# Hybrid decoder trunk: every gated mixture turned by VectorE squares and DRAM or made already turned, sparse half of the output projection first

## The reference, cut to what matters

```python
h = rms_norm(x, pre_w)
dq, dk, dv, dg, sq, sk, sv, sg, iq, ik, iw = split(h @ w_in)
# differential attention, 4 heads: two softmaxes, p0 - lam * p1, times dv
oa = rms_norm(diff_attention(dq, dk, dv, lam), subln_w) * (1 - lambda_init)
oa = oa * silu(dg)
# sparse attention, 4 heads of 128: 64 keys chosen per query by an indexer
ob = dsa_attention(sq, sk, sv, iq, ik, iw)     # softmax over the chosen keys
ob = ob * silu(sg)
y = concat([oa, ob]) @ w_out
x = x + rms_norm(y, post_w)
```

## Time and profile before

| what | value |
| --- | --- |
| median of 3 runs | 298.26 us (297.76 to 299.08) |
| the profiled execution, its own time | 297.96 us |
| its span in the trace | 296.2 us |
| TensorE busy | 289.2 us, 98% of the span |
| VectorE busy | 234.8 us, 79% |
| ScalarE busy | 164.5 us, 56% |
| GpSimd busy | 71.8 us, 24% |

### The profile page before, as it was taken

How to read it: one execution, slowest core, us unless ns; L and a number is a source line. 1 busy time by engine, 2 the same in 40 slices (tenths; PEclk the granted TensorE clock), 3 DMA queues, 4 the chain that set the end, 5 groups by cost and what they waited for, 6 DMA issues and landing times.

```text
span 296.2 us, 4373 instructions
## 1 busy us (share of the span) xinstructions
PE 289.2 (98%) x1544; PEld 244.2 (82%) x1544; DVE 234.8 (79%) x474; ACT 164.5 (56%) x284; POOL 71.8 (24%) x116
## 2 busy tenths in 40 slices
PE   8999999999999999999999999999999999999992
PEld 8799877788877888888888988778887788888892
DVE  4755889988978999957984686968898799999343
ACT  5988663736357685503666854473743949651101
POOL 6449510203304112001070740002312140210101
PEclk9999999999999999999999999999999999999999
DMA  7999968567665968993059796947768297764012
GB/s 252 370 365 394 388 218 318 171 153 240 140 259 81 339 169 210 219 307 118 1 169 371 235 358 152 388 152 198 229 134 292 37 285 249 187 117 123 0 71 71
DMA packets 77173, 63.15 MB, mean 213 GB/s; under 512 B 47200, under 2 KB 54112, under 8 KB 77152
## 3 DMA queue, kind: packets, MB, share of 16 engines
q1 hardware_dynamic: 76864, 62.62, 68.4%
q10 hardware_dynamic: 288, 0.26, 0.3%
HBM read 56.06 MB, written 6.82 MB: 212 GB/s over the span
## 4 chain that ended last, share of the span: by engine, by line
PE 95%; DMA 2%; SPq 1%; DVE 0%; ACT 0%; issue 0%; POOLq 0%; DVEq 0%; POOL 0%; ACTq 0%
PE bank_a L475 21%; PE bank_a L480 20%; PE bank_a L484 20%; PE bank_a L632 7%; PE bank_s L632 7%; PE bank_o L609 4%; PE bank_a L492 3%; PE bank_t L454 3%; PE bank_s L593 2%; DMA w_raw<-in_w_in 2%; PE bank_s L585 1%; PE bank_s L573 1%; PE bank_t L632 1%; PE bank_o L480 1%; PE bank_s L480 1%; PE bank_o L484 1%
## 5 line engine op out<-in xcount | busy, mean ns | idle before, releaser
L1002 DVE TENSOR_TENSOR w_lo<-w_raw,w_hi 128x2048 fp32r<-128x2048 f32 (+1 forms) x46 | 99.9, 2178 | 16.6 <-ACT w_hi L775 16.3
L775 ACT ACTIVATE w_hi<-w_raw 128x2048 fp32r<-128x2048 f32 (+1 forms) x46 | 81.9, 1786 | 28.4 <-PE bank_a L484 20.6
L475 PE MATMUL bank_a<-w_hi,h_hi 128*128 128x512 f32 (+1 forms) x272 | 72.2, 387 | 0.0
L480 PE MATMUL bank_a<-w_hi,h_lo 128*128 128x512 f32 (+1 forms) x272 | 69.9, 378 | 0.0
L484 PE MATMUL bank_a<-w_lo,h_hi 128*128 128x512 f32 (+1 forms) x272 | 69.8, 378 | 0.0
L480 PEld LDWEIGHTS bank_a<-w_hi,h_lo 128*128 128x128 f32 x272 | 49.8, 188 | 9.7
L484 PEld LDWEIGHTS bank_a<-w_lo,h_hi 128*128 128x128 f32 x272 | 49.7, 188 | 9.5
L475 PEld LDWEIGHTS bank_a<-w_hi,h_hi 128*128 128x128 f32 x272 | 48.1, 188 | 10.6 <-issue 2.6
L1445 POOL TENSOR_TENSOR rt<-nat,tab 128x256 f32<-128x256 f32 x10 | 8.6, 858 | 104.0 <-ACT nat L830 104.0
L830 ACT ACTIVATE nat<-bank_a,st 128x512 f32<-128x512 f32 x20 | 13.6, 686 | 30.7 <-PE bank_a L484 30.7
L846 ACT ACTIVATE xt_pbuf<-xt_pbuf,st 128x128 f32<-128x128 f32 (+1 forms) x48 | 21.2, 443 | 14.7 <-DVE st L1151 14.7
(11 more groups left out here) (198 smaller groups left out, 423.7 us busy)
## 6 DMA issues: line engine op xcount, KB each, us to landing
w_raw<-in_w_in SPq DMA_DIRECT2D x30, 1024.0 KB, 6.6
w_raw<-in_w_out SPq DMA_DIRECT2D x8, 1024.0 KB, 5.9
w_raw<-in_w_in SPq DMA_DIRECT2D x8, 584.0 KB, 7.3
turned<-mixn SPq DMA_DIRECT2D x28, 128.0 KB, 2.7
prm<-in_rows SPq DMA_DIRECT2D x2, 705.0 KB, 7.4
w_raw<-in_w_in SPq DMA_DIRECT2D x2, 512.0 KB, 6.3
xres<-in_x SPq DMA_DIRECT2D x2, 512.0 KB, 9.6
dqT<-turned SPq DMA_DIRECT2D x2, 512.0 KB, 5.9
```

Of the source, the lines that this page charges most:

```text
L475: pe.matmul(bank, h_hi[:, HALF * half + kk, tok], whi[:, kk, :], start=half == 0 and kk == 0, stop=False)
L480: pe.matmul(bank, h_lo[:, HALF * half + kk, tok], whi[:, kk, :], start=False, stop=False)
L775: act.activation(unit(w_hi, u), unit(raw, u), ACT.Copy).then_inc(hi_done.sem, 1)
L1002: dve.tensor_tensor(unit(w_lo, u), unit(raw, u), unit(w_hi, u).bitcast(F32), ALU.subtract).then_inc(lo_done.sem, 1)
```

## The change

- The gate chunk `SG` is computed turned: `turned_gate` takes the weights as the stationary operand and both blocks' tokens as the moving one, 256 columns a matmul. ScalarE moves it unscaled (`Copy`); the inverse roots `rx` are put into a DRAM row and read back to all partitions (`rx_rows`), GpSimd multiplies by them, and ScalarE applies SiLU later (`sparse_silu`).
- The sparse values are computed turned too: `values` swaps its operands for o 2 and 3. As an inverse sum can no longer be applied by partition to that output, the probabilities are normalised before they are turned: VectorE's `invert`, then GpSimd's multiply (`normed`), for uses 12, 13 and 14.
- `gate_dsa` multiplies the turned values with the turned gate and splits the result itself; nothing has to be turned.
- The differential mixture of block 0 goes by squares and DRAM as that of block 1 did (`MD0S`).
- The output takes the sparse half first: half 0 is now sparse and reads `h_hi`, `h_lo`; half 1 is differential. Units 20 to 23 hold the matrix in that order.
- The orders of VectorE, TensorE and SP at the end of a layer follow. `sparse_values_0` stands between `first(19)` and `second(19)`.

```diff
@@ scratch and buffers @@
-T_MD0, T_MS0, T_MS1 = 10, 11, 12
-T_USES = 13
-DKS, PS0, MD1S, PS1 = range(3, 7)
+T_USES = 10
+DKS, PS0, MD0S, MD1S, PS1 = range(3, 8)
+        rx_rows = sb("rx_rows", [P, SEQ])
+        sparse_gate = gate[:, :, 1, :].rearrange("p j (c t) -> p j c t", t=SEQ)
@@ SP @@
+            def put_mix(layer, b):
+                sp.wait_ge(mix_squares.sem, mix_squares.at(layer, b + 1))
+                put((MD0S, MD1S)[b], mix_buf[b], mix_put[b].sem)
+            def get_mix(layer, b):
+                sp.wait_ge(mix_put[b].sem, mix_put[b].at(layer, 16 * SQUARES))
+                sp.dma_start(mix_turned[b], ...).then_inc(mix_landed[b].sem, 16)
+                    if u == 4:
+                        sp.wait_ge(rx_ready.sem, rx_ready.at(layer, 2))
+                        sp.dma_start(scratch[-1][0, :].rearrange("(p b) -> p b", p=P), rx).then_inc(rx_put.sem, 16)
+                    if u == 5:
+                        sp.wait_ge(rx_put.sem, rx_put.at(layer, 16))
+                        sp.dma_start(rx_rows[:, :], scratch[-1].to_broadcast([P, SEQ])).then_inc(rx_landed.sem, 16)
...
                     if u == 0:
                         get_probs(layer, PS0)
+                        put_mix(layer, 0)
+                        put_probs(layer, PS1)
+                        get_mix(layer, 0)
+                        get_probs(layer, PS1)
+                        put_mix(layer, 1)
                     if u == 1:
-                        put_probs(layer, PS1)
-                        sp.wait_ge(mix_squares.sem, mix_squares.at(layer, 1))
-                        put(MD1S, mix_buf, mix_put.sem)
-                        get_probs(layer, PS1)
-                    if u == 2:
-                        sp.wait_ge(mix_put.sem, mix_put.at(layer, 16 * SQUARES))
-                        sp.dma_start(mix_turned, ...).then_inc(mix_landed.sem, 16)
+                        get_mix(layer, 1)
@@ TensorE @@
+                def turned_gate(layer, bank, u, pair, half):
+                    def products(w, x, first=False, last=False):
+                        for kk in range(HALF):
+                            for c in range(2):
+                                cols = slice((2 * pair + c) * P, (2 * pair + c + 1) * P)
+                                mm = pe.matmul(bank[:, c * SEQ:(c + 1) * SEQ], w[:, kk, cols], x[:, HALF * half + kk, :], ...)
+                        return mm
...
                 second(18)
-                turn_mix(T_MD0, 0, 0)
                 first(19)
+                sparse_values_0()
                 second(19)
-                pe.wait_ge(prob_landed[PS0].sem, prob_landed[PS0].at(layer, 16))
-                values(2, 0, v_dsa, ...)
-                pe.wait_ge(t_drained.sem, t_drained.at(layer, T_MD0 + 1))
+                pe.wait_ge(sparse_split.sem, sparse_split.at(layer, 1))
                 out_part(0, 0, 0)
-                turn_mix(T_MS0, 0, 2)
                 out_part(0, 0, 1)
-                pe.wait_ge(t_drained.sem, t_drained.at(layer, T_MS0 + 1))
-                out_part(1, 0, 0)
                 pe.wait_ge(prob_landed[PS1].sem, prob_landed[PS1].at(layer, 16))
                 values(3, 1, v_dsa, ...)
+                pe.wait_ge(mix_split.sem, mix_split.at(layer, 1))
+                out_part(1, 0, 0)
                 out_part(1, 0, 1).then_inc(y_done.sem, 1)
-                pe.wait_ge(mix_split.sem, mix_split.at(layer, 1))
+                pe.wait_ge(sparse_split.sem, sparse_split.at(layer, 2))
                 out_part(0, 1, 0).then_inc(out_unit_used.sem, 1)
-                turn_mix(T_MS1, 1, 3)
                 out_part(0, 1, 1).then_inc(out_unit_used.sem, 1)
-                pe.wait_ge(t_drained.sem, t_drained.at(layer, T_MS1 + 1))
+                pe.wait_ge(mix_split.sem, mix_split.at(layer, 2))
                 out_part(1, 1, 0).then_inc(out_unit_used.sem, 1)
@@ ScalarE @@
                 split_hi(layer, 13)
+                sparse_silu()
                 move(10)
@@ VectorE @@
+                def invert(use):
+                    r, n_rows = 4 * (use % 4), 4 if use == 12 else 2
+                    dve.wait_ge(exps_done.sem, exps_done.at(layer, use + 1 - S_DIFF0))
+                    dve.reciprocal(inv[:, r:r + n_rows], sums[:, r:r + n_rows]).then_inc(inverted.sem, 1)
                 def turn_probs(n, use):
-                    dve.wait_ge(exps_done.sem, exps_done.at(layer, use + 1 - S_DIFF0))
+                    dve.wait_ge(normed.sem, normed.at(layer, use + 1 - S_DSA0))
                 def gate_dsa(b):
+                    dve.wait_ge(sg_ready.sem, sg_ready.at(layer, 2))
                     dve.wait_ge(o_filled.sem, o_filled.at(layer, 3 + b))
-                    gated(2 + b, ...)
+                    dve.tensor_tensor(mixn[:, b, :]..., O[b][:, :]..., sparse_gate[:, :, :, tok], ALU.mult)
+                    link(dve.tensor_copy(h_hi[:, 0:HALF, tok], mix))
+                    dve.tensor_tensor(h_lo[:, 0:HALF, tok], mix, h_hi[...], ALU.subtract).then_inc(sparse_split.sem, 1)
...
                 choose(1, 2)
-                turn_probs(PS0, 12)
+                invert(12)
                 choose(1, 1)
                 mask_unchosen(1)
+                turn_probs(PS0, 12)
                 split_lo(layer, 19)
                 mask_scores(13, ...); mask_scores(14, ...)
                 gate_diff(0)
+                turn_mix(0)
+                invert(13)
+                invert(14)
                 split_lo(layer, 20)
                 turn_probs(PS1, 14)
                 gate_diff(1)
-                turn_mix()
-                drain_mix(T_MD0, m_hi, m_lo, 0, subln)
+                gate_dsa(0)
+                turn_mix(1)
                 split_lo(layer, 21)
-                gate_dsa(0)
+                split_mix(0)
                 split_lo(layer, 22)
-                drain_mix(T_MS0, h_hi, h_lo, 0)
+                gate_dsa(1)
                 split_lo(layer, 23)
-                split_mix()
-                gate_dsa(1)
+                split_mix(1)
                 weight_y(0)
                 residual(0)
-                drain_mix(T_MS1, h_hi, h_lo, 1)
@@ GpSimd @@
+                pool.wait_ge(rx_landed.sem, rx_landed.at(layer, 16))
+                for j in range(2):
+                    pool.wait_ge(proj_moved.sem, proj_moved.at(layer, place(layer, SG, j) + 1))
+                    pool.tensor_tensor(part, part, by_token.to_broadcast([P, 2, BLOCKS, P]), ALU.mult).then_inc(sg_scaled.sem, 1)
                 rope(DQ, 2 * HEADS, HD, 0)
...
                 for b in range(BLOCKS):
+                    for use in ((12,), (13, 14))[b]:
+                        pool.wait_ge(inverted.sem, inverted.at(layer, use + 1 - S_DSA0))
+                        pool.tensor_tensor(probs, probs, inv[:, r:r + n_rows][:, :, None].to_broadcast([P, n_rows, n]), ALU.mult).then_inc(normed.sem, 1)
                     pool.wait_ge(o_squared.sem, o_squared.at(layer, b + 1))
```

101 lines of the change are left out of this document (63 added, 38 removed).

## The result

The changed kernel takes 305.34 us (median of 6 runs, 304.12 to 306.07), against 298.51 us for the kernel before in the same session: ratio 1.022, 95% interval 1.020 to 1.024. It is slower by 6.8 us. Medians are of all executions; the ratios are of means, and leave out the one slow execution (over 1.5% above the fastest of its kernel) that experiments 6, 7 and 11 each had.

The account below looks back on a forecast made before the run. TensorE, busy for 98% of the span, was taken to bound the kernel. Turns -1.38, gate +0.6 and waits 4.5 gave +3.7 us a layer, +7.5 on 298.0: 305.5 us, 8-in-10 range 300.5 to 310.

Parts of the forecast that it names:

- Turned gate: TensorE's chunk SG: 96 matmuls of 256 columns replace 48 of 512, costing 0.6 us a layer more.
- Side work of the gate on GpSimd and ScalarE: GpSimd's two gate multiplies and ScalarE's Silus fall into idle time; without that cover they would cost 1.4 us.
- The two rx DMAs: In SP's queue before loads u=4 and u=5: a delay of a microsecond or two hides, at worst 1 us in layer 0.
- 0.55 before the sparse values: End of a layer: after first(19), TensorE waits 0.55 us for PS0 to land.
- 1.8 before the first output product: After second(19), TensorE waits 1.8 us for the sparse half, delayed by multiplies and split_lo(20) running one after the other.
- 0.25 for unit 21: After the first output product, TensorE waits 0.25 us for turn_mix(1) and split_lo(21) on VectorE.
- 0.3 before values(3): TensorE waits 0.3 us for PS1, taking 5.2 us from its first put to the get.
- 1.6 for unit 23: Before out_part(1,0,1), TensorE waits 1.6 us because split_lo(23) is queued behind gate_dsa(1) on VectorE.
- the multiplies don't meet the split: Rival: normed(14) ends at 260.7, only two waits a layer remain; 301 to 302 us, chance 0.18.
- slow multiply: Rival: GpSimd's multiply takes 2.4 us instead of 1.3, moving the chain 2.2 a layer; 310 us, chance 0.13.
- The turns decide: Rival: unit 23 comes within one product of values(3), PS0 and sparse half on time; 296.5 us, chance 0.03.
- Small waits only: Rival: the last wait is near 1.3 us and the others are covered; 298.5 to 299.7 us, chance 0.08.

Follow-up runs that it names:

- experiment 6: The changed kernel with unit 23's split ahead of gate_dsa(1), ScalarE scaling probabilities 13 and 14, and PS0's get issued ahead of unit 23's load: 302.12 us.
- experiment 7: The changed kernel with the two small rx DMAs issued from ScalarE's queue instead of SP's: 305.62 us.
- experiment 11: The kernel of experiment 10 with five turns of a constant tile, read by nobody, put back on TensorE: 302.28 us.
- experiment 1: The changed kernel with VectorE's split of unit 23 placed ahead of gate_dsa(1), nothing else: 301.97 us.
- experiment 2: The changed kernel without GpSimd's two multiplies for probabilities 13 and 14; VectorE's transpose waits for the exponentials instead: 302.29 us.
- experiment 5: The changed kernel with probabilities 13 and 14 scaled by ScalarE in place of GpSimd's two multiplies, nothing left out: 302.18 us.
- experiment 12: The kernel of experiment 9 with five turns of four identity tiles, read by nothing, added on TensorE: 300.47 us.
- experiment 10: The kernel of experiment 9 with SP's wait for the landed row of inverse roots moved from u=5 to u=7: 300.94 us.
- experiment 9: The changed kernel with both mends, unit 23's split ahead of gate_dsa(1) and ScalarE scaling probabilities 13 and 14: 298.71 us.
- experiment 4: The changed kernel without the two small DMAs for the inverse roots; GpSimd multiplies by ones instead: 304.65 us.
- experiment 8: The kernel of experiment 6 with the two rx DMAs issued from ScalarE's queue: 300.81 us.

## Why the prediction was right

The forecast was 305.5 us for the likeliest case, and 305.34 was measured. The direction and the two mechanisms that carry most of it, unit 23's split behind the gate and the multiplies that run one after the other with a split, are shown by experiments 1, 2 and 5. That the number came within 0.2 us is partly luck: the waits were put 2.5 us too high, 1.25 us of other losses were missed, and the 7.5 us were added to a single execution of 298.0 us, 0.5 below the median of the kernel before in the comparison. Point by point:

- **Turns removed, -1.38 a layer.** Right by experiment 12: 0.46 us each, in layer 0.
- **Turned gate, +0.6 a layer.** Right: 120 ns a matmul, 0.64 us by the start of layer 1's stretch (262.45 - 258.72 less the 3.09 us by which layer 1 began later).
- **Side work of the gate on GpSimd and ScalarE, hidden.** Right in the kernel after, where TensorE has no wait near them, but the cover is thinner than I said: I had GpSimd's idle 21.9 us as cover, and did not ask what VectorE does meanwhile. The trace of experiment 10 shows what happens when the first starts 1.8 us earlier than in 9 and `ik` is late.
- **The two rx DMAs, nothing, at worst 1 us.** Nothing contradicts the bound, but the reasoning failed: SP blocked for 8 us in layer 0 and not "a microsecond or two", since the 1 KB landed behind whole units. Experiment 4 gives 0.7 us for leaving them out, with intervals that overlap.
- **0.55 before the sparse values.** 0.53 in layer 1; none in layer 0, where PS0's get was issued 2.6 us ahead of `first(19)` (114.51 against 117.06) and in layer 1 1.8 (260.66 against 262.45).
- **1.8 before the first output product.** The term that was mis-sized: 0.7 in both layers. Multiplies and split take 4.2 us (261.64 to 265.81) and not 1.3 + 2.2 + 1.3 = 4.8, since a multiply is 1.04 us; they began 0.2 us earlier against the start of `first(19)`, and from their end to the sparse half it was 4.2 us (265.84 to 270.07) and not 4.5. Together 1.1 us: 1.8 - 1.1 = 0.7. That they run one after the other was right, the order (the split first) wasn't.
- **0.25 for unit 21.** Practically nothing (0.03). The prediction's own sum gives 0.1: 267.4 + 0.65 + 2.2 = 270.25, and not 270.35.
- **0.3 before values(3).** 0.45 and 0.76: PS1's get was 5.6 us behind its first put, not 5.2, and TensorE came to it earlier as the waits before were shorter.
- **1.6 for unit 23.** 1.65, in both layers; experiment 1 takes exactly this away.

So the waits are 6.5 us, where I had 9.0; the 2.5 us that are missing are partly made up by what I had not priced: 0.95 us in slow first rows behind waits, 0.3 us near 103 us. So the forecast for the span was +7.5 and the trace has +6.3. The medians differ by 6.8, nearer to the forecast, but no trace says where the other 0.5 us lie.

Of the rivals, "the multiplies don't meet the split" fell (GpSimd's row of 4.07 us), as did "slow multiply": 1.04 us, below the value that I took. The clock didn't fall in the kernel after. "The turns decide" would need unit 23 within one product: VectorE's rows from 278.44 to 282.53 are 4.1 us against 2.73. "Small waits only" fell with the last wait of 1.65 us and the ones beside it.

What stays open: why the first row behind a wait takes 0.1 us longer, whether the two `rx` DMAs cost anything, and if they do whether through the loads or through `iqT`; and why the kernels of experiments 6 to 11 scatter more from one execution to the next than the kernel before. No version measured here beats the kernel before; the best one, with both mends, equals it, since of the 2.8 us from the turns the gate takes 1.3 and the waits that are left some 1.4 with their slow first rows.

## What to carry to other kernels

Taking instructions off the engine that bounds a kernel pays only as long as its suppliers keep their lead: here 2.8 us of turns were saved, and two placements on other engines, a split behind a gate and two GpSimd multiplies beside a split, cost 6.6. For each new operation ask not only whether its own engine is idle, but what the engine that it excludes is doing, also in the stretches where it "hides": GpSimd's idle time is no cover where VectorE runs, at the same moment, work that TensorE waits for. And where a DMA stands in its queue is a change like any other: loads issued earlier cost 2.2 us in experiment 10, and one issued later, next to a transfer that TensorE waits for, 2.4 to 3.4 in experiment 6.

## What the runs showed of the hardware that I had not expected

- A 1 KB DMA took 10.6 us to land (median of the two in the kernel after) behind and between loads of 1 MB on the same queue, and from ScalarE's queue still 6.7 and 4.1 us. At the end of the span, with hardly any transfer beside them, two DMAs of 128 KB landed in 2.1 us (median). The Trainium skill, "DMA: Bandwidth & Descriptors", section "Issuing engines are not separate DMA queues", says that DMAs of the scalar, sync and gpsimd engines run on the same 16 DMA engines and interleave there. The 6.7 us agree with that: the DMA engines were over 90% busy in nearly all of that stretch (15 to 40 us). How much of the 10.5 us is the place in SP's queue no run separates.
- GpSimd's multiply of 128x512 took 1.04 us with no split beside it (VectorE's search ran beside one of them), less than the straight line through 128 and 256 elements gives (1.3); the gate's, with a second full operand, takes 1.31 us without one, and 3.41 and 3.31 in layer 1, where splits of 2.3 us start just ahead of it (182.74 against 182.79, 188.37 against 188.48).
- The meeting goes the other way too: a row of two small VectorE `tensor_scalar` (128x64) took 1.53 us and not 0.54 when a GpSimd multiply had started 0.06 us ahead of it (experiment 10 against 9).
- A wait of TensorE of 2.68 us was followed by a granted clock of 0.66 and 0.50 (1.2 GHz) over the next 4 us, a wait of 2.14 us in the same place of another kernel was not. Both are single executions.
- The first row of matmuls behind a wait takes about 0.1 us more than the same row without it.
